# Which engine makes the low parts of eight weight chunks: a change between GpSimd and VectorE

## The reference

```python
u = rms_norm(h, attn_norm[l])
proj = einsum('bsd,dc->bsc', u, w_in[l])            # 1024 x 7424
(dq, dk, dv, rq, rk, rv, rg, gq, gk, gv, gate_logits) = split_cols(proj, IN_SPLITS)
dq = partial_rope(rms_norm(dq, diff_q_norm[l]))      # differential queries, 512 columns
dk = partial_rope(rms_norm(dk, diff_k_norm[l]))      # differential keys, 512 columns
a = differential_attention(dq, dk, dv, lam)          # two softmaxes a head, 4 heads
r = bidirectional_retention(rq, rk, rv, ...)
c = grouped_query_attention(gq, gk, gv)              # 8 query heads, 2 key heads
h = h + einsum(merged(a, r, c, gates), w_out[l])
h = h + square(relu(rms_norm(h) @ w_mlp_in)) @ w_mlp_out
```

## Time and profile before

| | |
|---|---|
| median of 3 runs | 2929.67 us (2929.1 to 2929.99) |
| the profiled execution | 2929.27 us |
| its span | 2927.4 us |
| TensorE busy | 2877.2 us, 98% |
| VectorE busy | 1865.6 us, 64% |
| ScalarE busy | 1439.8 us, 49% |
| GpSimd busy | 306.7 us, 10% |
| mean granted clock of TensorE | 0.996 of full speed |

### The profile page before, as it was taken

How to read it: one execution, slowest core, us unless ns; L and a number is a source line. 1 busy time by engine, 2 the same in 40 slices (tenths; PEclk the granted TensorE clock), 3 DMA queues, 4 the chain that set the end, 5 groups by cost and what they waited for, 6 DMA issues and landing times. The chain is left out here.

```text
span 2927.4 us, 38315 instructions
## 1 busy us (share of the span) xinstructions
PE 2877.2 (98%) x14199; PEld 2330.7 (80%) x14199; DVE 1865.6 (64%) x2361; ACT 1439.8 (49%) x2120; POOL 306.7 (10%) x210
## 2 busy tenths in 40 slices
PE   8999999999999999999999999999999999999999
PEld 7887778888788887577778889897667777888988
DVE  4437768345864667666744787867756744587784
ACT  3557425234533456655553654445765554464442
POOL 5002300000100002211111000000221111000000
PEclk9999999999999999999999999999999999999999
DMA  7322223333333332123322433323222322433322
GB/s 190 94 75 71 60 58 94 97 97 96 106 90 104 94 101 68 49 80 87 94 72 87 123 101 101 95 80 94 62 61 73 109 73 79 123 101 101 101 87 72
DMA packets 407185, 263.45 MB, mean 90 GB/s; under 512 B 29674, under 2 KB 396124, under 8 KB 407008
## 3 DMA queue, kind: packets, MB, share of 16 engines
q1 hardware_dynamic: 401072, 250.09, 29.4%
q0 software_dynamic: 5936, 11.03, 1.4%
HBM read 253.70 MB, written 5.64 MB: 89 GB/s over the span
## 5 line engine op out<-in xcount | busy, mean ns | idle before, releaser
L751 DVE TENSOR_TENSOR wL<-wR,wH 128x1024 fp32r<-128x1024 f32 (+2 forms) x261 | 315.1, 1207 | 296.2 <-ACT wH L746 270.3
L826 PE MATMUL ps<-uH,wH 128*128 128x512 f32 x1184 | 477.5, 403 | 1.7 <-ACT wH L746 1.7
L826 PE MATMUL ps<-uL,wH 128*128 128x512 f32 x1184 | 462.9, 391 | 0.0
L746 ACT ACTIVATE wH<-wR 128x1024 fp32r<-128x1024 f32 (+3 forms) x352 | 361.6, 1027 | 179.6 <-DMA wR<-in_ffn_w_down_dram 53.2
L784 POOL TENSOR_TENSOR wL<-wR,wH 128x1024 fp32r<-128x1024 f32 (+1 forms) x91 | 222.6, 2448 | 1641.7 <-ACT wH L746 1639.0
L826 PE MATMUL ps<-uH,wL 128*128 128x512 f32 x1184 | 300.9, 396 | 0.0
L826 PEld LDWEIGHTS ps<-uH,wH 128*128 128x128 f32 x1184 | 223.2, 189 | 68.3 <-issue 21.0
L826 PEld LDWEIGHTS ps<-uL,wH 128*128 128x128 f32 x1184 | 223.2, 188 | 46.9 <-issue 3.2
L826 PEld LDWEIGHTS ps<-uH,wL 128*128 128x128 f32 x1184 | 219.7, 189 | 51.0 <-issue 6.1
L813 PE MATMUL ps<-uH,wH 128*128 128x512 f32 x528 | 208.3, 394 | 2.2 <-ACT wH L746 2.2
L813 PE MATMUL ps<-uL,wH 128*128 128x512 f32 x528 | 205.6, 389 | 0.0
(11 more groups left out here) (608 smaller groups left out, 6464.9 us busy)
## 6 DMA issues: line engine op xcount, KB each, us to landing
wR<-in_w_in_dram SPq DMA_DIRECT2D x182, 512.0 KB, 3.7
wR<-in_ffn_w_up_dram SPq DMA_DIRECT2D x44, 512.0 KB, 3.8
wR<-in_w_mlp_in_dram SPq DMA_DIRECT2D x22, 512.0 KB, 3.8
dn0R<-in_w_mlp_out_dram SPq DMA_DIRECT2D x22, 512.0 KB
dn1R<-in_w_mlp_out_dram SPq DMA_DIRECT2D x22, 512.0 KB, 3.4
dn2R<-in_w_mlp_out_dram SPq DMA_DIRECT2D x20, 512.0 KB, 3.4
wR<-in_w_branch_dram SPq DMA_DIRECT2D x16, 512.0 KB, 3.4
wR<-in_w_out_dram SPq DMA_DIRECT2D x16, 512.0 KB, 3.7
```

Of the source, the lines that this page charges most:

```text
L746: st.f(st.e.activation(wH[:, slot, 0:n], wR[:, slot, 0:n], ACT.Copy), hi_ready, c + 1)
L751: st.f(st.e.tensor_tensor(wL[:, slot, 0:n], wR[:, slot, 0:n], wH[:, slot, 0:n].bitcast(F32), ALU.subtract), lo_ready, c + 1 if done is Non ...
L826: ins = pe.matmul(o[:, :], w[:, k, :], x[:, k, :], start=s == 0, stop=s == 3 * KD - 1)
```

## The change

The set `BESIDE` loses the d chunks and keeps the dv chunks; all eight d chunks of each layer go into `ON_DVE`. Everything else follows from `by_pool`.

```diff
-BESIDE |= {_o[0].names[_name] for _o in ORDERS[1:] for _name in _o[0].names if _name[0] in ("d", "dv") and _name != ("d", 0)}
+BESIDE |= {_o[0].names[_name] for _o in ORDERS[1:] for _name in _o[0].names if _name[0] == "dv"}
+ON_DVE |= {_o[0].names["d", _t] for _o in ORDERS[1:] for _t in TILES["d"]}
```

## The result

| | before | after |
|---|---|---|
| median | 2929.06 us (2927.39 to 2929.99, 7 runs) | 2940.63 us (2938.18 to 2942.39, 7 runs) |
| the profiled execution | 2929.27 us | 2940.63 us |
| its span | 2927.4 us | 2938.8 us |
| mean granted clock of TensorE | 0.996 | 0.995 |

The changed kernel takes 1.0041 times as long, with a 95% interval of 1.0032 to 1.0051; that is 11.6 us by the medians, 9 to 15 by the interval. So it is slower, beyond the 0.2% that the measurement tells from no change.

A forecast was written before the change was run, and what follows sets the result against it. The limit was taken to be DVE's and ACT's order in the attention's softmax chain, which TensorE waits for. Two layers of 5.6 us add 11.2 us to the profiled 2929.27, giving a median of 2941 us, range 2932 to 2949.

The forecast's parts named there:

- DVE's queue stands behind ACT's high part: At d6 and d7, DVE waits 1.9 us for ACT's high part, works 1.3; maxima come 3.2 us later each.
- The slack of 0.9 us, spent once: TensorE's small product behind d6's exponential can absorb 0.9 us of delay, once a layer; later steps offer no such slack.
- d0, d4, d1, d5, d2 and d3 taken as 0.1 us together: Per layer, d0, d4, d1 and d5 cost 0, d2 gains 0.2 us, d3 loses 0.3 us.
- 5.6 us a layer: Net delay of TensorE in each layer's grouped-query attention: -0.2 + 3.2 + 0.3 + 3.2 - 0.9 us; 11.2 us in both.
- TensorE's waits of 12 to 13 us a layer: Sign expected in the trace: TensorE's waits in the attention stretch grow to near 12 to 13 us from 6.9.
- slack swallows it: Rival: TensorE loses only what exceeds the slack at each place, 2.7 to 5.4 us in all, 2932 to 2935; chance 0.17.
- the delays feed on each other: Rival: each delay moves ACT's next high part too; upper bound, +15 to +20 us, 2945 to 2949; chance 0.16.
- GpSimd's blocking was a cost: Rival: ending POOL's hold on DVE saves about 3.1 us of TensorE waits a layer, 2923.5 us; chance 0.05.

The follow-up runs named there:

- Run 2: As run 1, but at the old place DVE also waits for the same high part and does nothing there: 2944.52 us, ratio 1.0054.
- run 1: The changed kernel, but DVE makes each of the five single low parts one tile later, without a wait for ACT: 2929.75 us, ratio 1.0005.
- run 10: The change in the second layer only; the first layer keeps GpSimd's low parts: 2934.59 us, ratio 1.0024 to the kernel before.
- Run 4: The changed kernel, but the low parts of d6 and d7 stay on GpSimd; the other six go to DVE: 2928.79 us, ratio 1.0002.
- run 3: Only the low parts of d6 and d7 go to DVE; the other six stay on GpSimd: 2938.68 us, ratio 1.0038 to the kernel before.
- Run 7: The changed kernel, but each d low part is put off on DVE until right behind the next maxima: 2924.05 us, ratio 0.9985.
- Run 11: Low parts of d and three value chunks put off on DVE behind the next maxima; GpSimd works uselessly at eight single places a layer: 2923.47 us, ratio 0.9985.
- run 5: The changed kernel, but ACT makes a d chunk's high part before the root of the tile before, not behind it: 2929.41 us, ratio 1.0004.

## Why the prediction was right, and where it was not

**DVE's queue stands behind ACT's high part: right.** The two waits were put at 1.9 us and are 1.98; the maxima at d6 were put 3.2 us later and are 3.31. Run 2 shows that the wait brings the loss, run 1 that the work without it doesn't: what is left there is within 1.4 us (-1.2 to 4.1) of the kernel before.

**The slack of 0.9 us, spent once: right in size, wrong in place.** L2949 at 1174.24 starts at 1176.78, 2.5 us later: 3.3 less 0.8, as predicted. But the slack only puts the rest off. In run 10 the score products behind add it again, so that the shift has grown by 3.3 us before d7; at d7 the same happens once more (2.2 and 1.0). What does come off, 0.7 us, comes off further on, at a step where TensorE already waited in the kernel before. The prediction had looked at those steps and found no slack of that size in them. So 3.4 + 3.2 - 0.7, less 0.1 ahead of d6, is 5.8, where the prediction had 3.2 + 3.2 + 0.1 - 0.9 = 5.6; that the two corrections are of nearly one size is luck.

**d0, d4, d1, d5, d2 and d3 taken as 0.1 us together: right in the sum.** Run 4 has 0.45 us for these six in both layers (interval from -2.0 to 3.2). In detail it was off: d2 waits 1.03 us in the first layer instead of 0.5, and d3 not at all, since DVE comes to it 4.2 us later than before and ACT's high part only 3.2. In the second layer d2 waits 0.74 us and d3 0.92.

**5.6 us a layer: 6.7 measured in each, 5.8 in the layer of run 10 without half clock.** The term left out is TensorE's clock, which fell behind waits of over 2 us and was nowhere in the sum. It may be the 0.9 us between 5.8 and 6.7. But the layer with more half clock shifted by 0.3 us more than the other in run 2 and by 0.7 less in run 3, so how much of it is the clock stays open. The total, 11.2 forecast and 11.4 in the two profiled executions, fits better than its parts, and that is luck: 13.4 of the two layers less 2.0 us that are no effect of the change. The execution of before has half-clock stretches of 3.4 us near 1462 and 1722 us which that of after lacks, and there the shift falls by 1.7 and 0.3 us; such stretches come and go from one execution to the next, in other runs here too.

**TensorE's waits of 12 to 13 us a layer: too high**, 8.5 and 11.0. Part of the lost time shows as matmuls that take longer, and counts as busy; in the second layer of run 10, without half clock, the waits come to 11.6.

**The rivals.** That slack swallows it (2932 to 2935) falls with the result. That the delays feed on each other (2945 to 2949) falls too: behind the two places the shift doesn't grow, it shrinks. Its upper bound counted on value chunks that hold DVE where they missed it before; they held it before as well, for 2.81 us at 1202.22, and 2.75 after. That GpSimd's blocking was a cost (2923.5) was right about the chip and wrong about this change. Its condition was that the high parts are there when DVE comes for them; the change didn't meet it. Run 7 does, and gains 4.8 us against the kernel before on its chip, where the rival had 6.2; in its trace the two layers gain 3.3. The Trainium skill's page SBUF — State Buffer, section "Who interferes with whom", gives the rule for it (two-input DVE instructions and GpSimd's reads share one interface, and the second to start blocks). Run 11 agrees: GpSimd reading a table that has nothing to do with DVE's data makes DVE's two-input operations 1.42 us long instead of 0.69.

## What to carry to other kernels

An operation that moves from an idle engine to a busy one takes its wait with it, and the wait then holds all that is queued behind it: look up when its input is ready against when the new engine comes to it, before counting its work. The same low parts on DVE cost 11.6 us in one place of the queue and gained 4.8 in another; the good place is where the engine waits anyway and the input is old. Slack makes such costs jump: maxima that came 0.9 us late cost next to nothing (run 5), while behind those that came 3.3 us late the slack of 0.9 was lost again within two steps (run 10).

## What the chip showed beside this

TensorE's clock fell to half (1.2 GHz) for 3.4 or 6.8 us behind waits of 2.09 to 2.29 us in the middle of a stage in which it was otherwise busy, while after waits of 1.4 us in the same stage it stayed at 2.4 GHz. It didn't always fall: in the second layers of runs 2 and 10 it stayed at 2.4 GHz behind waits of 2.3 us. What decides was not tried. The price was between nothing and about 1 us a layer here, since slow matmuls used up time that TensorE would have waited.
